# A YOCO-style decoder step on one core: sample scores in four 32-column groups of TensorE, and the prompt's decay bias added by VectorE instead of TensorE

## What is computed

```python
s = q @ k.T * FOX_SCALE
logits = s + (cq[..., :, None] - cum_k[..., None, :])
p = softmax(where(kpos <= qpos, logits, -inf))
o = p @ v
```

## Time and profile before

| | us |
|---|---|
| median of 3 runs (1833.0 to 1834.33) | 1834.0 |
| the profiled execution, its own time | 1832.57 |
| its span | 1831.0 |
| attention stage, first score to the first product of the next projection (1101.6 to 1348.3) | 246.7 |

### The profile page before, as it was taken

The page is one execution under the profiler, slowest core; times in us unless marked ns, Lnnn a source line. Parts: engine busy times, 40 slices in busy tenths (PEclk is TensorE's granted clock), DMA queues, the critical chain, the costliest instruction groups (busy, mean ns, idle before and its releaser), DMA issues.

```text
span 1831.0 us, 33904 instructions
## 1 busy us (share of the span) xinstructions
PE 1771.3 (97%) x12818; PEld 1669.4 (91%) x12818; DVE 940.5 (51%) x1531; ACT 658.3 (36%) x1057; POOL 306.6 (17%) x347
## 2 busy tenths in 40 slices
PE   5999999989999999999999999999999999999997
PEld 5999999889999999999999996666679999999997
DVE  5888888864555555333444343333345555554221
ACT  4445545433333333222334452233234333333111
POOL 3222222312222221000000001000002122221000
PEclk8999999999999999999999998999999999999999
DMA  4222222212222222223333522363602222223331
GB/s 170 68 74 80 78 74 70 72 48 85 81 91 80 81 80 83 83 84 96 101 119 112 174 69 78 108 184 101 197 24 86 87 86 80 80 80 90 99 93 40
DMA packets 78372, 167.80 MB, mean 92 GB/s; under 512 B 6850, under 2 KB 40914, under 8 KB 78306
## 3 DMA queue, kind: packets, MB, share of 16 engines
q1 hardware_dynamic: 73218, 149.97, 26.8%
q0 software_dynamic: 5088, 16.93, 2.6%
HBM read 154.57 MB, written 12.30 MB: 91 GB/s over the span
## 4 chain that ended last, share of the span: by engine, by line
PE 93%; DVE 3%; issue 2%; ACT 1%; DMA 0%; SPq 0%; POOL 0%; DVEq 0%; ACTq 0%; POOLq 0%
PE acc L1351 73%; PE aux L1595 3%; PE aux L1378 3%; PE acc L1563 2%; PE acc L1582 2%; PE acc L1572 1%; PE acc L1565 1%; PE aux L1614 1%; PE aux L1511 1%; PE aux L1439 1%; PE aux L1432 1%; PE aux L1386 1%; DVE xl L714 1%; PE aux L1391 1%; PE aux L1417 0%
## 5 line engine op out<-in xcount | busy, mean ns | idle before, releaser
L1351 PE MATMUL acc<-xl,w_hi 128*128 128x288 f32 x2192 | 486.7, 304 | 22.0 <-DVE w_lo L708 15.5
L1351 PE MATMUL acc<-xh,w_lo 128*128 128x288 f32 x2192 | 470.6, 296 | 0.0
L1351 PE MATMUL acc<-xh,w_hi 128*128 128x288 f32 x2192 | 470.4, 296 | 0.0
L708 DVE TENSOR_TENSOR w_lo<-w_raw,w_hi 128x1024 fp32r<-128x1024 f32 (+1 forms) x217 | 283.1, 1304 | 336.4 <-ACT w_hi L383 333.3
L1351 PEld LDWEIGHTS acc<-xl,w_hi 128*128 128x128 f32 x2192 | 353.9, 190 | 35.6 <-DVE w_lo L708 16.1
L1351 PEld LDWEIGHTS acc<-xh,w_lo 128*128 128x128 f32 x2192 | 354.7, 190 | 0.0
L1351 PEld LDWEIGHTS acc<-xh,w_hi 128*128 128x128 f32 x2192 | 354.5, 189 | 0.0
L383 ACT ACTIVATE w_hi<-w_raw 128x1024 fp32r<-128x1024 f32 (+1 forms) x217 | 224.2, 1033 | 239.0 <-PE acc L1351 205.7
L1351 PE MATMUL acc<-ffn_glo,w_hi 128*128 128x288 f32 x704 | 151.1, 295 | 0.0
L1351 PE MATMUL acc<-ffn_gh,w_lo 128*128 128x288 f32 x704 | 149.8, 293 | 0.0
L1351 PE MATMUL acc<-ffn_gh,w_hi 128*128 128x288 f32 x704 | 148.9, 293 | 0.0
(11 more groups left out here) (254 smaller groups left out, 2570.5 us busy)
## 6 DMA issues: line engine op xcount, KB each, us to landing
w_raw<-w_fi_in SPq DMA_DIRECT2D x88, 512.0 KB, 3.6
w_raw<-w_mix_in SPq DMA_DIRECT2D x32, 512.0 KB, 3.6
w_raw<-w_fo_in SPq DMA_DIRECT2D x32, 512.0 KB, 3.5
dec_Kd<-cache_k_in SPq DMA_DIRECT2D x32, 512.0 KB, 6.6
dec_Vd<-cache_v_in SPq DMA_DIRECT2D x32, 512.0 KB, 5.5
w_raw<-w_kv_in SPq DMA_DIRECT2D x17, 512.0 KB, 3.7
w_raw<-w_o_in SPq DMA_DIRECT2D x16, 512.0 KB, 3.6
w_raw<-w_qg_in SPq DMA_DIRECT2D x16, 512.0 KB, 3.5
```

Of the source, the lines that this page charges most:

```text
L708: nc.vector.tensor_tensor(w_lo[:, pos.slot % SPL, 0:width], w_raw[:, pos.slot, 0:width], w_hi[:, pos.slot % SPL, 0:width].bitcast(F32), AL ...
L1351: mm = nc.tensor.matmul(acc[:, tp, hf, 0:HALF], W[:, sp_, 128 * j:128 * j + 128], X[:, kt, HALF * hf:HALF * hf + HALF], start=(first and j ...
```

## The change

PE's bias product, `cX` and `sel` go. POOL fetches, in place of `cX`, `NC`: minus `cum` of both heads, the same 4 KB row on each of 128 partitions (512 KB, two buffers). DVE's row maximum becomes one `tensor_tensor_reduce`, which reads the scores from PSUM and `NC` from SBUF, writes minus their sum back over the scores in PSUM, and takes the minimum along the row. ACT's exponent takes the sign back with scale -1. The wait for the transfer moves from PE, ahead of `score(0)`, to DVE, ahead of `mx(0)`. The transfer may start once DVE's `mx` of the turn before last is done (it was PE's score). An empty instruction that only increments `taking` stands ahead of each of the new reductions.

`Qb` shrinks to 8 x 32 columns: tile p = 2g + e belongs to column group g, and both tiles of a group accumulate into 32 rows of `D_ps`. Piece (half, e) of the sample scores is then four products, one to each group. POOL fills `Qb` with four copies of half the size in place of two. `cum` is written to DRAM once, as fp32 with its sign turned, in place of two parts. `cc` now lies in the buffer of `rms`. The mask table loses 256 of its columns.

```diff
-        c16h = t1("c16h", [FOX, T], F32R); c16l = t1("c16l", [FOX, T], F32R)
+        c16n = t1("c16n", [FOX, SEQ])
...
-        cX = t4("cX", [4, 2, SEQ], F32R)
-        sel = t4("sel", [4, 2, P], F32R)
+        NC = t4("NC", [P, 2, 2, SEQ])
...
-        Qb = t4("Qb", [P, 8 * 144]); Pd = t4("Pd", [P, T]); PTd = t4("PTd", [P, PAGES + 1, P])
-        cc = t4("cc", [P, T])
+        Qb = t4("Qb", [P, 8 * 32]); Pd = t4("Pd", [P, T]); PTd = t4("PTd", [P, PAGES + 1, P])
+        cc = rms
...
-                    nc.scalar.activation(Pr[:, x % 2, 0:w], S_ps(x % 2)[:, 0:w], ACT.Exp, bias=nm[:, x:x + 1],
+                    nc.scalar.activation(Pr[:, x % 2, 0:w], S_ps(x % 2)[:, 0:w], ACT.Exp, scale=-1.0, bias=nm[:, x:x + 1],
...
-            nc.vector.tensor_copy(c16h[:], c16[:]).then_inc(ch_ok, 1)
-            dve.wait_ge(ch_ok, 1)
-            nc.vector.tensor_tensor(c16l[:], c16[:], c16h[:].bitcast(F32), ALU.subtract).then_inc(cl_ok, 1)
+            nc.vector.tensor_scalar(c16n[:], c16[:, 0:SEQ], -1.0, None, ALU.mult).then_inc(cl_ok, 1)
...
                     dve.wait_ge(sc_ps, n + 1)
-                    nc.vector.tensor_reduce(nm[:, x:x + 1], S_ps(x % 2)[:, 0:w], AX.X, ALU.max, negate=True).then_inc(mx_ok, 1)
+                    nc.vector.sem_inc(taking, 1)
+                    s = S_ps(x % 2)[:, 0:w]
+                    nc.vector.tensor_tensor_reduce(out=s, in0=s, in1=NC[:, k, x // 4, 0:w], scale=-1.0, scalar=3.0e38,
+                                                   op0=ALU.add, op1=ALU.min, accum_out=nm[:, x:x + 1]).then_inc(mx_ok, 1)
...
                 if cur:
+                    dve.wait_ge(cx_in[k], 16 * (i // 2 + 1) if isinstance(i, int) else 8 * i + 16 - 8 * k)
                     mx(0)
...
-            nc.vector.tensor_copy(sel[:].rearrange("p a n -> p (a n)"), wide[0:4, 2 * P + NSEQ * NS:]).then_inc(zero_ok, 1)
             nc.vector.memset(Qb[:], 0.0).then_inc(zero_ok, 1)
...
-                wait(pool, sc_ps, 8 * (i - 1))
-                pool.dma_start(cX[:, k, :], d["c_row"][bass.ds(2 * i, 2)].rearrange("h e n -> (h e) n")).then_inc(cx_in[k], 16)
+                wait(pool, mx_ok, 8 * (i - 1))
+                pool.dma_start(NC[:, k], d["c_row"][bass.ds(2 * i, 2)].unsqueeze(0).to_broadcast([P, 2, SEQ])).then_inc(cx_in[k], 16)
...
-                    nc.gpsimd.tensor_copy(Qb[r, :].rearrange("p (k c) -> p k c", c=144)[:, :, 8 * a:8 * a + 8],
-                                          QT[r, :, bass.ds(SEQ + DSEQ * i, DSEQ)]).then_inc(qb_ok, 1)
+                    qb, qs = Qb[r, :].rearrange("p (g c) -> p g c", c=64), QT[r, :, bass.ds(SEQ + DSEQ * i, DSEQ)]
+                    qs = qs.rearrange("p (g e) t -> p g e t", e=2)
+                    for e in range(2):
+                        q = nc.gpsimd.tensor_copy(qb[:, :, 48 * e + 8 * a:48 * e + 8 * a + 8], qs[:, :, e, :])
+                    q.then_inc(qb_ok, 1)
...
-                    nc.tensor.matmul(s[:, w - P:w], idb, trib, start=False, stop=False)
-                    nc.tensor.matmul(s[:, 0:w], sel[:, a, :], cX[:, k, 0:w], start=False, stop=True).then_inc(sc_ps, 1)
+                    nc.tensor.matmul(s[:, w - P:w], idb, trib, start=False, stop=True).then_inc(sc_ps, 1)
...
-                        hf = piece // 2
-                        for p in range(4 * (piece % 2), 4 * (piece % 2) + 4):
-                            nc.tensor.matmul(D_ps[:, hf, 0:HALF], Qb[:, P * p:P * p + P], Kd[:, p, HALF * hf:HALF * hf + HALF],
-                                             start=(p == 0), stop=False)
+                        hf, e = piece // 2, piece % 2
+                        for g in range(4):
+                            p, r = 2 * g + e, slice(32 * g, 32 * g + 32)
+                            nc.tensor.matmul(D_ps[r, hf, 0:HALF], Qb[:, 32 * p:32 * p + 32], Kd[:, p, HALF * hf:HALF * hf + HALF],
+                                             start=(e == 0), stop=False, tile_position=(0, 32 * g))
```

More of the change, by code:

```diff
@@ L206, in build @@
         t6 = Region("wide", wide_at)
-        wide = t6("masks", [P, 4 * P + NSEQ * NS])
+        wide = t6("masks", [P, 2 * P + NSEQ * NS])
         t5 = Region("ao")
@@ L691, in _ @@
             att(0, True, False)
-            act.wait_ge(zero_ok, 5)
+            act.wait_ge(zero_ok, 4)
             att(1, True, True)
@@ L1043, in qg_pair @@
                     lo(Pos(B_QG + 1))
-                    dve.wait_ge(c_dram, 32)
+                    dve.wait_ge(c_dram, 16)
                     dve.wait_ge(v_out[0], 64)
@@ L1065, in _, with att @@
                 qg_pair(1, 2 * i + 1, i, 4)
-            def att(i, cur, prev):
+            def att(k, i, cur, prev):
                 def mx(x):
@@ L1149, in _ @@
             dve.wait_ge(ld_mask, 48)
-            nc.vector.tensor_copy(bfc[:], wide[:, 0:2 * P + NSEQ * NS]).then_inc(zero_ok, 1)
-            nc.vector.tensor_copy(sel[:].rearrange("p a n -> p (a n)"), wide[0:4, 2 * P + NSEQ * NS:]).then_inc(zero_ok, 1)
+            nc.vector.tensor_copy(bfc[:], wide[:]).then_inc(zero_ok, 1)
             nc.vector.memset(Qb[:], 0.0).then_inc(zero_ok, 1)
             dve.wait_ge(gt_ok, 8)
-            att(0, True, False)
-            att(1, True, True)
+            att(0, 0, True, False)
+            att(1, 1, True, True)
             with dve.Fori(1, 4) as i:
-                att(2 * i, True, True)
-                att(2 * i + 1, True, True)
-            att(8, False, True)
+                att(0, 2 * i, True, True)
+                att(1, 2 * i + 1, True, True)
+            att(0, 8, False, True)
             for p in range(DT):
@@ L1268, in _ @@
             pool.wait_ge(cl_ok, 1)
-            for e, part in enumerate((c16h, c16l)):
-                pool.dma_start(d["c_row"][:, e, :], part[:, 0:SEQ]).then_inc(c_dram, 16)
+            pool.dma_start(d["c_row"], c16n[:]).then_inc(c_dram, 16)
             def kv_pair(k, p):
@@ L1284, in _ @@
             pool.wait_ge(block_done, B_WO1)
-            pool.wait_ge(c_dram, 32)
+            pool.wait_ge(c_dram, 16)
             pool.wait_ge(kn_in, 1)
@@ L1309, in sample_queries @@
                     wait(pool, qb_ok, 2 * i + a)
-                    nc.gpsimd.tensor_copy(Qb[r, :].rearrange("p (k c) -> p k c", c=144)[:, :, 8 * a:8 * a + 8],
-                                          QT[r, :, bass.ds(SEQ + DSEQ * i, DSEQ)]).then_inc(qb_ok, 1)
+                    qb, qs = Qb[r, :].rearrange("p (g c) -> p g c", c=64), QT[r, :, bass.ds(SEQ + DSEQ * i, DSEQ)]
[3 more added lines that the diff above has]
+                    q.then_inc(qb_ok, 1)
             queries(0, 0)
-            pool.wait_ge(zero_ok, 3)
+            pool.wait_ge(zero_ok, 2)
             sample_queries(0)
@@ L1316, in _ @@
             nc.gpsimd.memset(QX[:, 1], 0.0).then_inc(zero_ok, 1)
+            pool.wait_ge(zero_ok, 3)
+            nc.gpsimd.memset(PTd[:], 0.0).then_inc(zero_ok, 1)
             pool.wait_ge(zero_ok, 4)
-            nc.gpsimd.memset(PTd[:], 0.0).then_inc(zero_ok, 1)
-            pool.wait_ge(zero_ok, 5)
             queries(1, 1)
@@ L1625, in att @@
                     pe.wait_ge(qx_ok, 2 * i + 2)
-                    pe.wait_ge(cx_in[k], 16 * (i // 2 + 1) if isinstance(i, int) else 8 * i + 16 - 8 * k)
                     score(0)
@@ L1676, in att @@
                     sample_scores(4)
-            pe.wait_ge(zero_ok, 3)
+            pe.wait_ge(zero_ok, 2)
             pe.wait_ge(ld_mask, 48)
@@ L1769 @@
     i = np.arange(P)
-    neg = np.zeros((P, 4 * P + NSEQ * NS), np.float32)
+    neg = np.zeros((P, 2 * P + NSEQ * NS), np.float32)
     neg[:, 0:P] = np.eye(P)
@@ L1774 @@
     own = (s_[None, None, :] // 8 == n_[None, :, None]) & (s_[None, None, :] % 8 <= i[:, None, None] % 8)
-    neg[:, 2 * P:2 * P + NSEQ * NS] = np.where(own, 0.0, -1e30).reshape(P, NSEQ * NS)
-    for a in range(2):
-        neg[2 * a:2 * a + 2, (a - 2) * P:(a - 1) * P or None] = -1.0
+    neg[:, 2 * P:] = np.where(own, 0.0, -1e30).reshape(P, NSEQ * NS)
     arrays["att_masks"] = neg
@@ L1785 @@
     d |= {k: nc.dram_tensor(f"{k}_out", s, F32, kind="ExternalOutput").ap() for k, s in outs.items()}
-    d["c_row"] = nc.dram_tensor("c_row", (FOX, 2, SEQ), F32R, kind="Internal").ap()
+    d["c_row"] = nc.dram_tensor("c_row", (FOX, SEQ), F32, kind="Internal").ap()
     build(nc, d)
```

## The result

The changed kernel takes 1780.7 us (median of 4 runs, 1779.7 to 1782.4) against 1834.1 before: a ratio of 0.971, 95% interval 0.969 to 0.973, 53 us less. 1779 was forecast, with 1767 to 1797.

What follows compares the result with a forecast made beforehand. PE was taken to bound the kernel, with the keys' transfer ending last after the change. Seven turns save 47 us, turn 0 and the start 8, together 55: 1832.6 becomes 1777.6, plus 1.4 gives 1779 us, range 1767 to 1797.

Steps and rivals of the forecast that it cites:

- PE is the bound, and the keys come next: Attention stage: PE nearly full, 28.6 of 30 us; after the change the keys' transfer ends last, by 1.1 us.
- A piece of the sample scores: Sample scores on PE: a piece as one set of four column groups takes 0.63 us in place of 1.94.
- The gain of the pieces: Sample scores on PE: 1.31 us gained for a piece, 5.2 us a turn.
- Rival C: Sample scores: changing between full width and 32 columns costs more; lone set 1.0 us, 1790 us in all; chance 0.07.
- Bias products: All eight leave PE: 2.7 us a turn gained, with 0 to 0.8 us a turn given back as ends.
- NC: Its transfer amid the key pages: keys land 11.6 us after the request, against 10.2; ends 10.2 and 14.1.
- Rival A: Keys' transfer: the new transfer fits gaps, keys land at 10.2 us, PE binds, 1773 us in all; chance 0.14.
- B: Keys' transfer: the new transfer is slow and costs the keys 3.9 us; turn 25.3 us, 1795 in all; chance 0.08.
- The maximum: Fused row maximum on DVE: same length plus 0.1 us, ends 0 and +0.4, hidden behind other PE work.
- Turn 0: First turn of the stage, with its keys early: 7 us gained in it.
- The sum: Whole kernel: turns of 23.0 us give 47 us in seven, first turn and start 8, together 55; 1779 us.
- E, the clock in part of each turn: TensorE: 3.4 us of each turn at 1.2 GHz, each turn 1.7 us longer, 1793 us in all; chance 0.05.

## Why the prediction was right

- *PE is the bound, and the keys come next.* Right. The keys' transfer ends last in six turns, by 1.5 us (1.1 forecast), and both kernels that free it save the time.
- *A piece of the sample scores.* 0.62 us, forecast 0.63, but the term left out what the product behind it pays, 0.20 us. The reckoning took its 0.15 from rows in which sets follow each other and never looked at the score behind a set. The chain of the kernel before had the price in it. These are two scores of 512 keys, the first behind the values' product in column groups, the second behind a piece of full width:

```profile
1228.32 1.06 PE acc L1563 x2
...
1245.30 0.86 PE acc L1563 x2
```

- *The gain of the pieces.* 4.5 us a turn by this, not 5.2. Rival C, a costlier change of width, is partly true: 0.82 us for a lone set, half of the surplus that it had put in. The prediction looked for the price in the 0.27 us ahead of the first set, and counts two changes in a turn where there are four (into and out of two runs of sets).
- *Bias products.* 3.1 us a turn, not 2.7. The step that failed is the bound "0 to 0.8 us given back": nothing was given back by PE, the transposes right behind a mask product became 0.15 us faster in each of six steps (0.9 us), and 0.5 went into waits. Behind the first piece the two errors nearly cancel (0.8 lost on four scores, 0.6 gained on four sets of transposes): 11.4 us to the next request against 11.2.
- *NC.* Keys at 12.4 us against 11.6. Of the 0.8 between them 0.5 is the base: 10.2 was read from one turn, and the mean of the seven turns of that profile is 10.7. The rest is the addition, 1.7 in place of 1.4. Rival A is out, and B at its price of 3.9; that the repeated row costs something, 0.5 us, is what one execution says.
- *The maximum.* The operation itself is as forecast (0.70 us for 512 columns), but its result comes later than "plus 0.1": the reduction starts 0.16 us later behind the score, and a readout of the minimum (its own row, 0.14 us, most of it behind the reduction) follows. Some 0.25 us in all, within the range of 0 to 0.4. That it is hidden was only half right, and the sign "no wait of PE for the exponent over 0.2 us" failed: loads wait up to 0.5. With the keys early a turn takes 22.8, not the 21.8 of PE alone, and the experiment with the longer maxima shows three steps without cover, one of which had none in the kernel before. The cover of "1.8 us against 1.55" was too thin for what was hung on it. As long as the keys come last, most of this is hidden behind their wait.
- *The wait on DVE.* Nothing, as said: no wait of DVE for NC stands among the waits.
- *Turn 0.* 11 us in place of 7, and 2.5 of it is the clock's length in the first profile of before, which differs from run to run: against the second profile turn 0 gives 8.5. The rest was not looked into.
- *The sum.* 23.6 us a turn for 23.0 forecast, 43.0 us for 47; turn 0 and the start 11.9 for 8. Together 54.8 for 55: near to exact by terms that were each off by 4 us in opposite directions. The mechanism was right; that the total fits so closely is luck.
- *E, the clock in part of each turn.* Seen in one of the fourteen turns of its two profiles. But with 1.5 us more of waiting it is real, in all six turns with the second transfer. The chance of 0.05 was for a mechanism that stood 1.5 us of waiting away.

## What to carry to other kernels

When an engine is sped up in a loop, look for the transfers whose request hangs on its own progress: their slack shrinks by as much as the loop does, and a new transfer issued at the same signal takes what is left. Such a transfer is best asked for when the urgent one has landed, which here cost one wait on an idle engine and gave 6 to 7 us. Work cut in column groups should be put in runs, since each change of width has a price that stands in the row of the product behind it (shown on the kernel before, not tried on the changed one); and the lengthening of a link between engines is to be measured from signal to signal, not by the row of the instruction.

## What was not expected of the hardware

- A product of full width that follows products of 32 columns takes 0.20 us more, whatever its length (128 to 512 columns), and the entry 0.13 us (0.62 for a lone piece, 1.11 for two in a row).
- Transposes of fp32 behind a float32r product took 0.15 us longer than behind a bf16 product.
- With an empty instruction on VectorE that only increments a semaphore ahead of it, and the wait on that, the new reduction started 0.20 us behind PE's product, where the old one without it took 0.04; five more put it off by 0.47, so 0.09 each. What the rest of the first 0.16 is, the operation or the wait, is not shown.
- Waits of PE for the keys of 1.5 us in the mean left TensorE at 2.4 GHz in eleven of twelve turns; waits of 3.0 us in the mean took it to 1.2 GHz in all six.
- A transfer that reads one row of DRAM 128 times delayed the keys by 1.7 us, one of the same size from 128 rows by 1.2, in one execution whose turns spread over 1.2 us. Whether the row is the cause is open.
